# Final norm: all rows beside the last two experts, their rows a second time by index

## The reference, cut to what matters

```python
x = x + concat(ya, yb) @ w_out                  # mixers and residual
h2 = rmsnorm(x, norm2_g)
eidx, gates = hier_route(h2, ...)               # top 2 of 32 experts for each row
x = x + moe_ffn(h2, eidx, gates, w1, w3, w2)    # sum of gate * (silu(h2 @ w1) * (h2 @ w3)) @ w2
y_prompt, y_sample = rmsnorm(xp, normf_g), rmsnorm(xs, normf_g)
# rmsnorm(x, g) = x * rsqrt(mean(x * x) + EPS) * g, row by row
```

## Time and profile before

| | |
|---|---|
| median of 3 runs | 964.62 us |
| profiled execution | 957.51 us |
| its span | 955.7 us |
| PE busy | 883.1 us, 92% |
| DVE, ACT, POOL busy | 29%, 11%, 16% |
| read from and written to HBM | 240.33 MB and 25.04 MB |

### The profile page before, as it was taken

One profiled execution on the slowest core, in us unless ns is written; L12 is line 12 of the kernel. 1 busy time (PEld: TensorE's weight loads), 2 busy tenths in 40 slices (PEclk: granted clock), 3 DMA queues, 4 the chain that ended last, 5 costly groups with the idle time before them and its releaser, 6 DMA issues. The chain is left out here.

```text
span 955.7 us, 28225 instructions
## 1 busy us (share of the span) xinstructions
PE 883.1 (92%) x12202; PEld 637.1 (67%) x12202; DVE 280.4 (29%) x839; ACT 102.9 (11%) x159; POOL 155.6 (16%) x262
## 2 busy tenths in 40 slices
PE   5899999999999997899999999999999799999940
PEld 2757758576684854867768686868686576767620
DVE  2544656547465454350010101010101001010106
ACT  1110110101011013001001010101010010100003
POOL 1000100000000011212212222222222122223110
PEclk9999999999999997799999999999999999999985
DMA  8780200201021029699999999999999999999948
GB/s 335 242 311 1 90 23 22 88 0 44 0 88 45 3 90 340 241 397 402 392 394 408 389 410 387 409 389 407 389 408 388 408 401 395 406 393 400 399 152 320
DMA packets 57390, 258.10 MB, mean 270 GB/s; under 512 B 10643, under 2 KB 11723, under 8 KB 40436
## 3 DMA queue, kind: packets, MB, share of 16 engines
q1 hardware_dynamic: 47436, 237.98, 61.9%
q0 software_dynamic: 9264, 19.32, 8.1%
q10 hardware_dynamic: 640, 0.07, 0.1%
HBM read 240.33 MB, written 25.04 MB: 278 GB/s over the span
## 5 line engine op out<-in xcount | busy, mean ns | idle before, releaser
L1413 PEld LDWEIGHTS ps<-hT,big 128*64 128x64 f32 x8192 | 292.4, 139 | 36.1 <-issue 34.7
L1413 PE MATMUL ps<-hT,big 128*64 128x80 f32 (+2 forms) x8192 | 297.8, 235 | 11.8 <-issue 10.7
L1434 PE MATMUL ps<-big,poolT 128*80 128x512 f32 (+2 forms) x512 | 191.4, 594 | 1.0 <-issue 0.6
L1167 DVE TENSOR_TENSOR poolT<-u,ps 128x320 f32<-128x320 f32 (+2 forms) x32 | 15.5, 486 | 405.1 <-PE ps L1413 405.1
L1434 PEld LDWEIGHTS ps<-big,poolT 128*80 128x80 f32 (+2 forms) x512 | 64.3, 149 | 103.9 <-issue 101.6
L1285 PEld LDWEIGHTS ps<-hT,big 128*64 128x64 f32 x2048 | 111.5, 137 | 7.0 <-issue 6.1
L1285 PE MATMUL ps<-hT,big 128*64 128x128 f32 x2048 | 115.3, 273 | 0.0
L591 POOL DMA_INDIRECT x_rows<-xn,sidx x22 | 32.9, 1496 | 263.3 <-ACT xn L799 253.1
L568 POOL DMA_INDIRECT slot_table<-ids,dest x18 | 18.7, 1037 | 302.7 <-DVE dest L916 300.0
L1272 PE MATMUL ps<-big,hT 128*128 128x512 f32 x128 | 59.8, 620 | 3.0 <-DMA big<-in_w_in 1.6
L1354 PE MATMUL ps<-big 128*128 128x512 f32 x128 | 56.9, 598 | 1.5 <-DVE big L1037 1.5
(11 more groups left out here) (205 smaller groups left out, 573.3 us busy)
## 6 DMA issues: line engine op xcount, KB each, us to landing
big<-in_exp_w SPq DMA_DIRECT2D x192, 1024.0 KB, 23.4
big<-in_w_in SPq DMA_DIRECT2D x4, 1536.0 KB, 12.8
big<-in_w_out SPq DMA_DIRECT2D x2, 2048.0 KB, 17.8
x_rows<-big SPq DMA_DIRECT2D x8, 512.0 KB, 2.6
h_rows<-xn SPq DMA_DIRECT2D x8, 512.0 KB, 2.9
big<-x_rows SPq DMA_DIRECT2D x8, 512.0 KB, 6.9
out_y_prompt<-big SPq DMA_DIRECT2D x8, 512.0 KB, 2.8
big<-in_x_prompt SPq DMA_DIRECT2D x1, 3072.0 KB, 11.2
```

Of the source, the lines that this page charges most:

```text
L1413: last = pe.matmul(out[c * w:(c + 1) * w, j, 0:m], up_weights(n)[:, k, j * P + c * w:j * P + (c + 1) * w], xT[:, 4 * half + k, 0:m], start ...
L1434: last = pe.matmul(ps[first:first + m, 5 + cols, :], hhT[:, 2 * half + k, 0:m], down_weights(n)[:, k, cols * 512:(cols + 1) * 512], start= ...
```

## The change

`x3` now lies over the chunks of set 2, which block 29 was the last to use. SP loads the nine tiles (`load_rows`) as soon as the scatters of blocks 0 to 29 have landed and PE has used block 29's weights, in its list right behind the last weight chunk of block 31. ACT takes the squares of tiles 0 to 2 between its two instructions for block 30 and those for block 31, and of tiles 3 to 8 between the silu and the result of block 31. DVE norms the tiles in groups of 2, 3 and 4 (`TILE_GROUPS`): the first behind block 30's product, the second behind block 31's product, the third behind block 31's result. SP stores each as before.

The tiles so stored lack what blocks 30 and 31 add. So POOL holds back the scatters of blocks 30 and 31 until all nine tiles have been loaded (`x3_in`), and after each of them it waits for its landing and gathers the same rows of `x3_rows` again (`gather_sum`) into the block's `xg`. ACT squares these rows, DVE norms them (`norm_late`), and POOL writes them to the outputs by index (`scatter_out`): one DMA for `y_prompt` and one for `y_sample`, where the indices that lie outside are left out. The index of a sample row is made by DVE (`gidx`). Both `scatter_out` wait until all nine tiles are stored, and the second also until the first has landed. The loop for the case of `over` loads, norms and stores all rows once more.

```diff
+TILE_GROUPS = (range(0, 2), range(2, 5), range(5, NT))
+FREE = 30
+LATE = NE - FREE
...
-        x3 = [big[:, j * D:(j + 1) * D] for j in range(NT)]
+        x3 = [big[:, third + j * D:third + (j + 1) * D] for j in range(NT)]
...
+            def load_rows():
+                for j in range(NT):
+                    m = P if j < LAST else NS
+                    sp.dma_start(x3[j][0:m, :], x3_rows[P * j:P * j + m, :]).then_inc(x3_in[j], 16)
...
+            for s in range(SETS):
+                sp.wait_ge(rows_out[s], 16 * len(range(s, FREE, SETS)))
+            sp.wait_ge(used, CH * FREE)
+            load_rows()
+            store_rows(0)
             sp.wait_ge(plan_ready, 1)
             over = sp.value_load(plan[0:1, 2 * MAXO:2 * MAXO + 1], min_val=0, max_val=MAXO)
+            sp.wait_ge(y_stored, 16 * NT)
+            for s in range(len(FINAL_CAPS) - LATE, len(FINAL_CAPS)):
+                sp.wait_ge(rows_out[s], 16 * (FINAL + 1 + 2))
             with sp.If(over > 0):
...
-
...
-            for s in range(SETS):
-                sp.wait_ge(rows_out[s], 16 * len(range(s, NE, SETS)))
-            sp.wait_ge(ov_free, over + 1)
-            for j in range(NT):
-                m = P if j < LAST else NS
-                sp.dma_start(x3[j][0:m, :], x3_rows[P * j:P * j + m, :]).then_inc(x3_in[j], 16)
...
-            sp.wait_ge(y_stored, 16 * NT)
+                sp.wait_ge(ov_free, over + 1)
+                load_rows()
+                store_rows(1)
+                sp.wait_ge(y_stored, 16 * 2 * NT)
...
+            def gather_sum(dst, idx, done):
+                pool.indirect_dma_start(
+                    dst, None, x3_rows, bass.IndirectOffsetOnAxis(ap=idx.bitcast(U32), axis=0),
+                    bounds_check=last_row, oob_is_err=False).then_inc(done, 16)
+
+            def scatter_out(src, idx, idx_sample, done):
+                pool.indirect_dma_start(
+                    y_prompt[0], bass.IndirectOffsetOnAxis(ap=idx.bitcast(U32), axis=0), src, None,
+                    bounds_check=last_prompt, oob_is_err=False).then_inc(done, 16)
+                pool.indirect_dma_start(
+                    y_sample.rearrange("b s d -> (b s) d"),
+                    bass.IndirectOffsetOnAxis(ap=idx_sample.bitcast(U32), axis=0), src, None,
+                    bounds_check=last_sample, oob_is_err=False).then_inc(done, 16)
...
                         pool.wait_ge(y_half_ready, h)
+                    if isinstance(b, int) and b >= FREE:
+                        for j in range(NT):
+                            pool.wait_ge(x3_in[j], 16)
                     pool.wait_ge(y_ready, count)
                     scatter_add(ys[s][0:m, :], sidx[s][0:m, :], rows_out[s])
+                    if isinstance(b, int) and b >= FREE:
+                        pool.wait_ge(xgT_done, NE)
+                        pool.wait_ge(rows_out[s], h * 16 + 16)
+                        gather_sum(xg[s][0:m, :], sidx[s][0:m, :], rows_in[s])
...
-            for s in range(SETS):
-                pool.wait_ge(rows_out[s], 16 * len(range(s, NE, SETS)))
+            pool.wait_ge(numbered, 4)
+            pool.wait_ge(xn_ready, NT + 1)
+            pool.wait_ge(y_stored, 16 * NT)
+            scatter_out(xg[0][0:FINAL_CAPS[0], :], sidx[0][0:FINAL_CAPS[0], :], gidx[0][0:FINAL_CAPS[0], :], rows_out[0])
+            pool.wait_ge(numbered, 3 + LATE)
+            pool.wait_ge(x2n_ready, NT + 1)
+            pool.wait_ge(y_stored, 16 * NT)
+            for s in range(LATE - 1):
+                pool.wait_ge(rows_out[s], 16 * (FINAL + 1 + 2))
+            scatter_out(xg[1][0:FINAL_CAPS[1], :], sidx[1][0:FINAL_CAPS[1], :], gidx[1][0:FINAL_CAPS[1], :], rows_out[1])
             pool.wait_ge(plan_ready, 1)
...
+            for s in range(len(FINAL_CAPS) - LATE, len(FINAL_CAPS)):
+                pool.wait_ge(rows_out[s], 16 * (FINAL + 1 + 2))
             pool.memset(oidx[:, :], 0).then_inc(ov_free, 1)
...
+            def square_tiles(tiles, turn=0):
+                for j in tiles:
+                    m = P if j < LAST else NS
+                    act.wait_ge(x3_in[j], 16 * turn + 16)
+                    reached(act, sq3, turn * NT + j)
+                    if turn + j == 0:
+                        act.wait_ge(ssf_set, 2)
+                    act.activation(junk[0:m, :], x3[j][0:m, :], ACT.Square,
+                                   accum_out=ssf[0:m, 0, j:j + 1]).then_inc(sq3, 1)
...
                     act.wait_ge(used, b * CH + 2)
                     act.activation(s1T[:, :, 0:m], up1[:, :, 0:m], ACT.Silu).then_inc(silu_done, 1)
+                    if isinstance(b, int) and b == NE - 1:
+                        square_tiles(range(3, NT))
                     act.wait_ge(used, b * CH + CH)
...
+                    if isinstance(b, int) and b == NE - 2:
+                        square_tiles(range(0, 3))
 
             triples(act, block_triple)
-
+            act.wait_ge(rows_in[0], 16 * (FINAL + 2))
+            act.wait_ge(sq3, NT)
+            m = FINAL_CAPS[0]
+            act.activation(junk[0:m, :], xg[0][0:m, :], ACT.Square, accum_out=ss1[0:m, 0:1]).then_inc(sq1, 1)
+            act.wait_ge(sq1, NT + 1)
+            act.wait_ge(rows_in[1], 16 * (FINAL + 2))
+            m = FINAL_CAPS[1]
+            act.activation(junk[0:m, :], xg[1][0:m, :], ACT.Square, accum_out=ss2[0:m, 0:1]).then_inc(sq2, 1)
+
...
-
-            for j in range(NT):
-                m = P if j < LAST else NS
-                act.wait_ge(x3_in[j], 16)
...
+                square_tiles(range(NT), 1)
...
+            def norm_tiles(turn, tiles, past=0):
+                dve.wait_ge(sq3, past + tiles[-1] + 1)
+                w = ssf[:, :, tiles[0]:tiles[-1] + 1]
+                rstd(w, w[:, 0:1], 1.0 / D, rs3_step, turn, rs3, several=True)
+                dve.wait_ge(rs3, turn + 1)
+                for j in tiles:
+                    m = P if j < LAST else NS
+                    dve.scalar_tensor_tensor(x3[j][0:m, :], x3[j][0:m, :], ssf[0:m, 1, j:j + 1],
+                                             gf[0:m, :], ALU.mult, ALU.mult).then_inc(y_out, 1)
+
+            def norm_late(s, w, squares, step, rs, ready):
+                m = FINAL_CAPS[s]
+                dve.wait_ge(sidx_ready, FINAL * SETS + s + 1)
+                dve.wait_ge(rows_in[s], 16 * (FINAL + 2))
...
+                dve.tensor_scalar(gidx[s][0:m, :], sidx[s][0:m, :], SEQ, None, ALU.bitwise_xor).then_inc(numbered, 1)
+                dve.wait_ge(squares, NT + 1)
+                rstd(w[0:m, :], w[0:m, 0:1], 1.0 / D, step, NT, rs)
+                dve.wait_ge(rs, NT + 1)
+                dve.scalar_tensor_tensor(xg[s][0:m, :], xg[s][0:m, :], w[0:m, 1:2], gf[0:m, :],
+                                         ALU.mult, ALU.mult).then_inc(ready, 1)
...
             def block_triple(h, caps_of):
                 for s, m in enumerate(caps_of):
                     b = h * SETS + s
+                    if isinstance(b, int) and b == FINAL * SETS:
+                        dve.memset(ssf[:, :, :], 1.0).then_inc(ssf_set, 1)
+                        dve.wait_ge(in_gf, 16)
+                        dve.tensor_scalar(gf[:, :], gf[:, :], NEWTON, None, ALU.mult).then_inc(ssf_set, 1)
+                        dve.wait_ge(ssf_set, 2)
                     dve.wait_ge(silu_done, b + 1)
                     dve.wait_ge(used, b * CH + 4)
                     dve.tensor_tensor(hhT[:, :, 0:m], s1T[:, :, 0:m], up3[:, :, 0:m], ALU.mult).then_inc(hhT_ready, 1)
                     if not isinstance(b, int) or b + 1 < NE:
                         take_xgT(b + 1, caps_of[(s + 1) % len(caps_of)])
+                    if isinstance(b, int) and b >= FREE:
+                        norm_tiles(s, TILE_GROUPS[s])
                     if in_halves(m):
...
             triples(dve, block_triple)
+            norm_tiles(2, TILE_GROUPS[2])
+            norm_late(0, ss1, sq1, rs1_step, rs1, xn_ready)
+            norm_late(1, ss2, sq2, rs2_step, rs2, x2n_ready)
...
-            for turn, tiles in enumerate((range(0, 3), range(3, 6), range(6, NT))):
-                norm_tiles(turn, tiles)
+                for n, tiles in enumerate(TILE_GROUPS):
+                    norm_tiles(len(TILE_GROUPS) + n, tiles, NT)
```

More of the change, by code:

```diff
@@ L501, in _, with store_rows @@
             load_weights(FINAL, len(FINAL_CAPS))
+            def load_rows():
+                for j in range(NT):
+                    m = P if j < LAST else NS
+                    sp.dma_start(x3[j][0:m, :], x3_rows[P * j:P * j + m, :]).then_inc(x3_in[j], 16)
+            def store_rows(turn):
+                for j in range(NT):
+                    sp.wait_ge(y_out, turn * NT + j + 1)
+                    dst, m = (y_prompt[0, j * P:(j + 1) * P, :], P) if j < LAST else \
+                        (y_sample.rearrange("b s d -> (b s) d"), NS)
+                    sp.dma_start(dst, x3[j][0:m, :]).then_inc(y_stored, 16)
+            for s in range(SETS):
[3 more added lines that the diff above has]
```

(30 more changed lines are left out.)

6 lines of the change are left out of this document (2 added, 4 removed).

## The result

The changed kernel takes 975.67 us at the median (973.87 to 976.83, 4 runs) against 964.26 us (961.88 to 968.83, 4 runs) of the kernel before beside it: ratio 1.0098, 95% interval 1.0065 to 1.013. It is 11.4 us slower; 5.9 were forecast. The profiled execution takes 974.52 us with a span of 972.9.

A forecast was written before the change was run, and what follows sets the result against it. The tail after block 31's result, 35.1 us with PE idle, was taken to bound it: result 20.6 us later, 20.4 following instead of 35.1, so 5.9 us lost on the 964.62 median: 970.5 us, range 962 to 978.

The forecast's parts named there:

- the sum's own range: Whole kernel: the summed steps give 970.5 us, own range 966.5 to 974.5; chance 0.46.
- the third rival: New tail: small DMAs land as slowly as beside weights, giving 977; chance 0.18 with anything else priced too low.
- the 0.5 us that lie between the last landing and the end before: Kernel's end: 0.5 us from last landing, 961.1, to end of span, 961.6.
- the 917.7: Line of weights ahead of the rows: ends at 914 on most DMA engines, 917.7 on the last.
- the last tile: Loads of the nine tiles behind the weights: taken as 11 us, all in at 927.0.
- The down projection: PE's part of block 31: at half clock after standing still, 7.8 us, ending at 934.7.
- Block 30's scatter: POOL's list after the tiles: starts at 927.9, takes 6.0 us to land, at 933.9.
- the gates: POOL's gather of block 31's gates: issued at 937.2, 3.3 us to land, deciding block 31's result at 941.2.
- the last gather: POOL's gather of block 31's rows after its scatter: starts 948.4, lands 4.1 us later at 952.5.
- 1 (indirect DMAs as fast as plain ones): POOL's tail: quiet rows land in 2.8 us, gates in 2.1; 964.8, no change; chance 0.22.
- 2 (rows not behind the weights): Tile loads: packets alternate with weights, tiles in by some 919; 962.5; chance 0.11, half of it no change.
- 4 (PE's stall shows): Block 31's result: gates land before 934.7, so it waits for half-clock PE; at most 2 us; chance 0.03.

The follow-up runs named there:

- third experiment: The changed kernel run again without an edit, beside the kernel before: 974.89 us, ratio 1.0165.
- first trace after: Profiled execution of the changed kernel in the main measurement, no further edit: 974.52 us, span 972.9.
- second experiment: The kernel before with one added wait, so POOL ends its list only when all nine tiles are stored: 969.27 us, ratio 1.0101.
- second trace of before: The kernel before, unchanged, profiled once more: 960.20 us, ratio 1.0005.
- 72 more: The kernel before with POOL ending last, plus 72 small indirect DMAs issued by POOL beside the attention part: 1183.13 us, ratio 1.2217.

## Why the prediction was short by half

The direction and the chain were right. The 975.67 us lie within the stated range by luck: the sum's own range ended at 974.5, and the room above it was made for the third rival, which did not come about. The steps of the forecast beside the trace of the changed kernel at before's pace (the third experiment), and the first trace after:

| step | forecast | same pace | first trace |
|---|---|---|---|
| block 29's scatter starts (given) | 891.95 | 891.18 | 904.33 |
| first tile squared | near 919 | 914.2 | 920.0 |
| block 31's silu | 923.2 | 919.4 | 923.5 |
| PE's down projection ends | 934.7 | 929.4 | 933.4 |
| tiles in, block 30's scatter starts | 927.9 | 927.7 | 930.3 |
| block 31's gates issued | 937.2 | 937.6 | 938.4 |
| block 31's result done | 941.2 | 940.6 | 942.1 |
| block 31's scatter starts | 942.1 | 941.5 | 943.1 |
| last gather starts | 948.4 | 946.9 | 948.5 |
| last output scatter starts | 958.8 | 959.2 | 960.3 |
| last landing | 961.1 | 961.6 | 962.6 |
| end of the span | 961.6 | 971.9 | 972.9 |

**The step that failed** is "the 0.5 us that lie between the last landing and the end before". It was read off a kernel that ends with SP's stores; the term for POOL's DRAIN was put at nothing. From POOL's last landing to the end it is 961.6 to 971.9, 10.3 us. The difference at the same pace, 971.9 - 955.7 = 16.2, is 6.1 to the start of the DRAIN (forecast 5.9) and 10.1 of DRAIN and end. The second experiment shows that cost by itself (9.5 us). It was to be seen beforehand: the row stood in the trace of before, under line L83, which the timeline leaves out. The Trainium skill ("VectorE: DVE Perf Modes", section "The DRAIN you can't avoid") calls the DRAINs at a kernel's end boilerplate of about 12 ns on all engines; SP's 13 ns agree, POOL's 9382 and 9872 ns don't, nor do PE's 2255.

**Terms that were off and cancelled.** In the third experiment the last weight chunk was issued at 888.4 and landed 24.5 us later, at 912.9, and the first tile landed at 914.2 (13.8 behind its issue). So the rows did stand behind the weights, but the line ended 5 us before the 917.7 that the sum took from one late DMA engine in the trace of before; the second trace of before has 915.3 there. Nearly 14 us then passed to the last tile instead of 11, and the two cancelled. The windows of the third experiment, columns as in the earlier trace rows:

```profile
912.00:914.00 2.00, 2.00 (x76) 2.00 (x72) 0.00 (x0) 0.00 (x0) 0.00 (x0) 1.00 1.01 404
914.00:916.00 2.00, 0.41 (x14) 0.27 (x10) 0.00 (x0) 1.15 (x2) 0.00 (x0) 1.00 1.05 412
...
918.00:920.00 2.00, 0.00 (x0) 0.00 (x0) 1.44 (x9) 1.91 (x6) 0.00 (x0) 0.50 0.92 365
```

The DMA share stays near 1 past 914, where it fell to 0.33 before, and the granted clock falls to 0.50, the 1.2 GHz level, once PE has been without work since 914.4. The down projection took 6.0 us instead of 7.8: it ran at 0.50 up to 928 and at 1.00 from 928.5 on, and at full clock the whole of it is 3.65 (first trace after), not 3.9. It ended 10 us before the result was written. Block 30's scatter took 7.1 us to land, not 6.0; block 31's 4.6, not 5.5; the gates 2.2, not 3.3; the last gather, though nearly alone, 5.7, not 4.1. They cancel: the last landing was forecast at 961.1, and the DRAIN starts at 961.8.

**The rivals.** 1 (indirect DMAs as fast as plain ones) fell for scatters that add (7.1 and 4.6) and for the gather (5.7), and for the output scatters too, if by less: they landed 3.2 (rows) and 2.3 and 3.0 us (samples) behind their issue, about where the sum had them. 2 (rows not behind the weights) fell at before's pace: the scatter was released at 927.7, not by 921. At the other pace block 30's scatter starts 26.0 us behind block 29's instead of 36.5, which needs no turns with the weights: SP issues the rows 21.3 us behind its last weights there (890.9 to 912.14) and 10.6 here (889.7 to 900.33), so less of the line is left in front of them. 3 (the new tail isn't quiet) didn't come about: beside the stores the landings were some longer and some shorter than forecast, and the price of 977 is near the measured time for another reason. 4 (PE's stall shows) fell; the first trace has no half-clock stretch there at all, its gap being 2.35 us, and is no faster.

**What the change's idea was worth.** It trades a tail of 35.1 us for two costs that the experiments separate. The second pass over the last rows costs 15 to 20 us: 14.7 by two traces of one pace, from block 29's scatter to the DRAIN (58.5 against 43.8), and 20.0 by the medians' differences to before in two jobs (11.4 + 8.6), whose kernels before differ by 2.9. The hold costs up to 8.7, of which 1.2 is the scatter that doesn't add. Without either, at a price in outputs, it was 17.2 under before, in the job in which before was slowest. No kernel that computes all rows came out faster than before.

**How much slower it is depends on the loop's pace.** Before's median was 959.77, 959.05, 964.26 and 967.12 in four jobs; the changed kernel's 974.89 and 975.67 in two of them, a difference of 15.1 and 11.4. Traces of both tails at both paces are there, from block 29's scatter to POOL's DRAIN:

| tail | 47.8 us per three blocks | 49.0 |
|---|---|---|
| before, POOL last | 62.6 (second experiment) | 62.8 (72 more) |
| changed | 70.6 (third experiment) | 58.5 (first trace after) |

Before's tail takes the same time at either pace. The changed one is 12.1 us shorter at the slower pace; the issue times under rival 2 say why, its rows find less of the weights in front of them. So at the slower pace the change does shorten the way to the DRAIN, by 4.3 us, and loses by the exposed DRAIN; at the faster it loses by both. An estimate from this: to the end of the span it is 68.6 us from block 29's scatter in the first trace after and 63.8 in that of before, so at the slower pace the change would cost some 5 us, near the forecast but made of other terms. No trace of before as it stands was taken at that pace. Which pace a run has goes with the chip in these traces: the six of the first and last job, on two chips, have 47.8, and the four of the job between, on a third, have 49.0 (for the first two traces the chip isn't on record). What sets it stays open.

## What to carry over

- Read what every engine does at the very end, the instructions that a timeline leaves out too: a DRAIN of 9 to 10 us on the engine that issues software DMAs costs nothing while its list ends early, and all of it as soon as its last DMA is the kernel's last.
- Work that is taken from the tail by way of indirect DMAs comes back as a chain of them, 5 to 8 us from start to start here for rows that are added or gathered; count the links before the bytes.
- Before a difference of two traces is explained, compare a stage ahead of the change: 12.4 us of one difference here were there already.

## What had not been expected of the hardware

- POOL's DRAIN at the end of its list took 9382 ns (the kernels with 114 indirect DMAs), 9872 (120), 8725 and 8729 (138 and 186, the extra ones early) and 6606 (138, the extra ones last), each the same to the nanosecond in every trace of a kind; landings had all come before it.
- An indirect DMA of 128 four-byte elements, 512 bytes in all, cost the kernel 2.1 to 2.9 us in both places where it was put. Beside the attention part PE's matmuls came one per 2.8 us with "issue" as the only reason; at the end the stores of 512 KB took a median of 63.3 us to land instead of 2.8. That these are one cause isn't shown. Busy DMA engines don't explain the first (share 0.01 there); in the second their share is at its full while they move 32 GB/s. Why stays open.
- The same kernel ran its expert loop at 47.8 us per three blocks in one trace and at 49.0 in another; all traces of one chip had the same pace, where the chip is on record. How long the mixers take differed too, by up to 3 us between two traces of the kernel before.
